# Moving the residual sums before the second FFN from GpSimd's program to VectorE's, in a decoder layer on one core

## What is computed

```
h = x + 0.5 * rms(swiglu(rms(x, g)), g)                 # first FFN
u = rms(h, g);  merged = gateA * attention(u) + gateB * recurrence(u)
h = h + rms(merged @ w_out, mix_post_g)                 # the sum that this case is about
h = h + 0.5 * rms(swiglu(rms(h, ffn2_pre_g)), g)        # second FFN
rms(y, g) = y * rsqrt(mean(y*y) + eps) * g
```

## Time and profile before

| | |
|---|---|
| runs | 2288.19 us median (2286.82, 2288.19, 2291.76) |
| profiled execution | 2288.33 us, span 2286.5 us |
| TensorE busy | 2158.2 us, 94% of the span |
| VectorE busy | 1389.8 us, 61% |
| ScalarE busy | 974.8 us, 43% |
| GpSimd busy | 450.2 us, 20% |
| mean granted clock of TensorE | 0.979 |

### The profile page before, as it was taken

One profiled execution on the slowest core, in us unless ns is written; L12 is line 12 of the kernel. 1 busy time (PEld: TensorE's weight loads), 2 busy tenths in 40 slices (PEclk: granted clock), 3 DMA queues, 4 the chain that ended last, 5 costly groups with the idle time before them and its releaser, 6 DMA issues.

```text
span 2286.5 us, 25908 instructions
## 1 busy us (share of the span) xinstructions
PE 2158.2 (94%) x9837; PEld 1789.6 (78%) x9837; DVE 1389.8 (61%) x1718; ACT 974.8 (43%) x1543; POOL 450.2 (20%) x453
## 2 busy tenths in 40 slices
PE   4999999999998999999999888998699999999997
PEld 3888788878886888888887777776588888888885
DVE  7668865557576666212214887677856766557666
ACT  5333333344353776311324666445433333334343
POOL 5123320000032221000012555215312321000012
PEclk8999999999999999999999999999799999999998
DMA  3345442253442212222310100455135453216334
GB/s 120 93 156 185 157 166 70 70 198 98 151 148 80 57 46 54 69 70 85 106 43 25 27 14 10 166 189 175 55 98 185 164 197 123 72 51 221 101 134 142
DMA packets 220293, 249.85 MB, mean 109 GB/s; under 512 B 24261, under 2 KB 161546, under 8 KB 220170
## 3 DMA queue, kind: packets, MB, share of 16 engines
q1 hardware_dynamic: 220170, 248.19, 33.3%
HBM read 192.06 MB, written 55.57 MB: 108 GB/s over the span
## 4 chain that ended last, share of the span: by engine, by line
PE 85%; DVE 6%; ACT 3%; POOL 2%; issue 2%; DMA 1%; POOLq 0%; SPq 0%; ACTq 0%; DVEq 0%
PE ps L88 28%; PE ps L90 27%; PE ps L89 27%; PE ps L2172 1%; PE ps L2140 1%; DVE ff_t L98 1%; POOL a_rot L2057 1%; PE ps L357 1%; ACT a_probs L2116 1%; DVE a_s L2106 1%; DVE a_pt L98 1%; DVE entry_y L342 0%; DVE w_lo L98 0%; DMA w_raw<-in_w_out_dram 0%; ACT entry_squares L282 0%
## 5 line engine op out<-in xcount | busy, mean ns | idle before, releaser
L98 DVE TENSOR_TENSOR ff_w_lo<-ff_raw,ff_w_hi 128x512 fp32r<-128x512 f32 x264 | 209.8, 798 | 171.9 <-ACT ff_w_hi L94 171.8
L88 PE MATMUL ps<-ff_t,ff_w_hi 128*128 128x512 f32 x704 | 276.4, 393 | 18.8 <-DVE ff_t L98 18.8
L89 PE MATMUL ps<-ff_t,ff_w_hi 128*128 128x512 f32 x704 | 275.9, 392 | 0.0
L90 PE MATMUL ps<-ff_t,ff_w_lo 128*128 128x512 f32 x704 | 275.6, 392 | 0.0
L94 ACT ACTIVATE ff_w_hi<-ff_raw 128x512 fp32r<-128x512 f32 x264 | 164.9, 627 | 180.7 <-PE ps L90 173.5
L88 PE MATMUL ps<-d_b_hi,d_a_hi 128*128 128x512 f32 x608 | 237.5, 391 | 3.7 <-DVE d_a_lo L98 3.7
L98 DVE TENSOR_TENSOR w_lo<-w_raw,w_hi 128x1024 fp32r<-128x1024 f32 (+2 forms) x81 | 93.9, 1164 | 237.1 <-ACT w_hi L94 237.0
L90 PE MATMUL ps<-d_b_hi,d_a_lo 128*128 128x512 f32 x608 | 236.7, 389 | 0.0
L89 PE MATMUL ps<-d_b_lo,d_a_hi 128*128 128x512 f32 x608 | 236.7, 389 | 0.0
L88 PE MATMUL ps<-ff_b,ff_w_hi 128*128 128x512 f32 x528 | 209.6, 397 | 8.1 <-ACT ff_u2x L692 5.0
L90 PE MATMUL ps<-ff_b,ff_w_lo 128*128 128x512 f32 x528 | 208.2, 394 | 0.0
(11 more groups left out here) (296 smaller groups left out, 4365.7 us busy)
## 6 DMA issues: line engine op xcount, KB each, us to landing
ff_raw<-in_ffn_w_gate_dram SPq DMA_DIRECT2D x44, 512.0 KB, 4.0
ff_raw<-in_ffn_w_up_dram SPq DMA_DIRECT2D x44, 512.0 KB, 4.0
d_sums<-in_ffn_w_down_dram SPq DMA_DIRECT2D x44, 512.0 KB, 4.1
sums_scratch<-d_sums SPq DMA_DIRECT2D x88, 256.0 KB, 2.6
w_raw<-in_w_in_dram SPq DMA_DIRECT2D x32, 512.0 KB, 4.0
d_raw<-sums_scratch SPq DMA_DIRECT2D x24, 512.0 KB, 3.3
w_raw<-in_w_out_dram SPq DMA_DIRECT2D x24, 512.0 KB, 4.3
spill_scratch<-ff_st SPq DMA_DIRECT2D x44, 256.0 KB, 3.1
```

What stands on the lines that cost most here:

```text
L88: pe.matmul(out, lh, rh, start=start, stop=False, skip_group_check=go_on)
L89: pe.matmul(out, lh, rl, start=False, stop=False, skip_group_check=go_on)
L90: return pe.matmul(out, ll, rh, start=False, stop=stop, skip_group_check=go_on)
L98: return nc.vector.tensor_tensor(lo, src, as_f32(hi), ALU.subtract)
```

## The change

The flag `add` of `norm_pool` and `norm_dve` says which of the two issues the sum of step 2. For the tiles 0 to 4, which are handled beside groups 1 and 2 of the output projection, GpSimd's program is now told not to (it had the default, True), and VectorE's is told to (it had the default, False). The other calls stay.

```diff
--- before.py
+++ after.py
@@ -2864,7 +2864,7 @@
                 for g in range(1, 3):
                     for k in range(DK):
                         for s, q in out_steps(g, k):
-                            entry(f2, s, q)
+                            entry(f2, s, q, False)
                 for z in range(11):
                     for s, q in row(z, 5, NT):
                         entry(f2, s, q, False)
@@ -2993,7 +2993,7 @@
                                 op.evacuate_dve(dve, t)
                         if g > 0:
                             for s, q in out_steps(g, k):
-                                entry(f2, s, q)
+                                entry(f2, s, q, True)
                         if k < 6 and 8 + 8 * g + k + 3 < len(outs):
                             w.lo(dve, outs[8 + 8 * g + k + 3])
                     if g < 2:
```

## The result

| | before | changed |
|---|---|---|
| median of 20 runs | 2287.98 us | 2292.79 us |
| ratio, 95% interval | | 1.0023 (1.0016 to 1.0030) |
| profiled execution, span | 2288.33, 2286.5 us | 2288.75, 2287.0 us |

The ratio compares all executions of the two kernels and is not the quotient of the two medians; one of the 20 executions of before took 4893 us and is left out of it (without that one the median of before is 2287.76 us). By the ratio the change makes the kernel slower by 0.23%, which is 5.3 us (3.7 to 6.9); by the medians it is 4.8 to 5.0 us. The forecast was +4.1 us, 2292.3. The likeliest of the three classes had been "no change within 0.2%" at 0.54 against 0.42 for slower; the measured ratio lies 0.03% on the other side of that bound, but the bound is inside its interval, so the timing does not decide between the two.

A forecast was written before the change was run, and what follows sets the result against it. TensorE is 94% busy; in output projection group 2 a ring of ScalarE, GpSimd and VectorE steps sets the time. 0.3 + 2.5 + 0.1 + 1.9 - 0.7 = +4.1 us on 2288.2 gives 2292.3, range 2289.5 to 2295.2.

The forecast's parts named there:

- the three terms of group 2: Output projection group 2: later sums of tiles 2, 3 and 4, at +2.5, +0.1 and +1.9 us.
- The clock term: PE's slow clock after its waits: less of it falls on matmuls, -0.7 us, bounds -1.9 and +1.7.
- Tiles 0 and 1, +0.3: Group 1: sums later in VectorE's queue delay PE's tail of group 1 by 0.3 us, bounds 0 and +0.4.
- Tile 2, +2.5: Group 2: the sum queues behind a w_lo waiting for PE-released w_hi, so its square starts 2.5 us later.
- Tile 3, +0.1: Group 2: pre-gain of tile 2, then the sum, take 2.45 us from the root's end; +0.1 us.
- Tile 4, +1.9: Group 2: sum behind w_lo, low part, pre-gain and GpSimd's whole at the port; +1.9 us, bounds +0.8 and +2.1.
- Rival C: VectorE goes first at the port, so tile 4 costs +0.8; all in all +3.0 us, 2291.2; chance 0.13.
- rival B: The clock gives nothing back or takes more: +4.8 to +6.5 us, 2293.0 to 2294.7; chance 0.25.
- The signs of being wrong: Tile 2's square before 1576, tile 4's sum taking 1.2, or slow stretches moving by more than a microsecond.
- Rival D, the faster engine: VectorE's sum is 1.17 us shorter, twice in the chain: -2.3 us, 2285.9; chance 0.12 shared with another rival.

The follow-up runs named there:

- Run 3: Only the sums of tiles 0 and 1 moved from GpSimd to VectorE, against the kernel before; median 2287.01 us, ratio 0.9994.
- run 2: Only the sum of tile 4 moved from GpSimd to VectorE, against the kernel before; median 2290.65 us, ratio 1.0011.
- run 8: Only tile 4's sum on VectorE, ahead of the pre-gain of tile 3 instead of behind it; against the kernel before, median 2288.16 us, ratio 1.0001.
- run 1: Only the sum of tile 2 moved from GpSimd to VectorE, against the kernel before; median 2291.24 us, ratio 1.0009.
- run 5: Changed kernel with the sums of tiles 0 and 2 directly behind their own post-gain; against the kernel before, median 2289.86 us, ratio 1.0010.
- run 4: Changed kernel with all five sums on VectorE directly behind their own post-gain; against the kernel before, median 2283.79 us, ratio 0.9978.
- run 7: All sums stay on GpSimd, each ahead of the root of the tile before; against the kernel before, median 2290.07 us, ratio 1.0010.

## Why the prediction was right

The time, 2292.79, is 0.5 us from the forecast, and in the changed kernel's profile the three terms of group 2 came out on the paths that were given for them. The clock term did not hold, the path at tiles 0 and 1 was another, and the 0.5 us is less than the timing can tell.

*Tiles 0 and 1, +0.3.* The distance from post-gain to tail grew by 0.57, but not on the path that I gave, over VectorE's own queue: the w_lo now waits 1.57 us for a w_hi, and that for a load, as this row of ScalarE shows. The load was issued at 1540.12 and used at 1545.92, 5.8 us later, where before it took 4.5.

```profile
1545.92 1.06 ACT L94 ACTIVATE w_hi<-w_raw 128x1024 fp32r<-128x1024 f32 x1 [3.15 <-DMA w_raw<-in_w_out_dram]
```

The prediction named this load and took it as 0.4 late. It is issued hardly later (12.87 us behind the post-gain of tile 0, before 12.75) but takes longer: 5.6 to 5.9 us from issue to use in the three profiles with these two sums on VectorE in step 2, 4.5 to 5.1 where group 1 is that of before. Why it takes longer no run shows. Run 3 (ratio 0.9994) and the scatter of this group in runs 2 and 8 leave the term unproved; it is small either way.

*Tile 2, +2.5.* 2.52 in the changed kernel, 2.50 in run 1, and 0 in run 5, where only the place is undone. *Tile 3, +0.1.* 0.12. *Tile 4, +1.9.* 1.79, and 1.77 in run 2; that the whole goes first at the port is seen in the 2.29 of the sum there, in run 5 too, and in the 1.22 of run 8, where the sum stands ahead of the whole. Rival C is out. The waits of PE came as said, 3.21 before the turn of tile 3 (3.3 forecast); before that of tile 4 it is 1.41, not over 2, since the chunk ahead of it ran slow (granted clock 0.50), which the prediction had weighed under rival B and called hidden in that wait. It was: the piece up to the tail is 9.40, before 9.42.

The Trainium skill (SBUF — State Buffer, Who interferes with whom) gives the port to the instruction issued first, for its whole length; the trace agrees in both directions, GpSimd's sum held by w_lo (3.31) and VectorE's held by whole (2.29).

*Clock, -0.7.* The profile has +1.46 before the w_hi, -1.58 in the tail and -0.5 after it, -0.6 in all. But run 1 has the same late w_hi, with the same program ahead of it, and across the ten profiles the distance from restart to w_hi goes from 4.42 to 7.33. Before stands between the two, so in one execution the clock moves the time by 1.5 us either way, and over many it need not give anything back. That this one profile shows -0.6 beside the -0.7 of the prediction is chance. The timed 5.3 us (3.7 to 6.9) has room for 4.1 and lies nearer to the terms without the clock, which measured 0.57 + 4.41 = 5.0. If a term was mis-sized it is this one; what it is over many executions no run shows.

*The signs of being wrong.* Two of the three that the prediction names came up. The square of tile 2 starts at 1574.95, before 1576; this says nothing, since that execution reached the post-gain of tile 0 3.95 us early, and absolute times of two executions should not have been compared. The slow stretches did move by more than a microsecond, twice and in opposite directions (+1.46 and -1.58); this one counts, against the clock term. The third, a sum of tile 4 of 1.2, did not.

*Rival D, the faster engine.* It falls for this change, but run 4 shows that it named something real: with the sums on VectorE and put where their inputs are ready, the ruler is 2.7 us shorter and the kernel 5.0 us faster, and run 7 shows that GpSimd's sums, put early, do not give that. How much of it is the shorter sum and how much the relief of the port was not taken apart. My condition for it, that tile 2's w_hi be released sooner, was too narrow; it is enough to put the sum on the other side of the w_lo.

## What to carry to other kernels

Moving an instruction to a faster engine moves it into another queue. Ask what stands ahead of it there and what that waits for: here a sum of 1.22 us cost 2.5 us behind a w_lo that waited for TensorE, and nothing in front of it. When work changes engines, place it anew by when its inputs are ready and its result is wanted; here another order turned 5 us lost into 5 us gained, with the same instructions on the same engines. And measure a change this small as a distance between two events of the chain: single executions of the kernel before lay between 2283.64 and 2291.76 us, which is more than the effect. The distance leaves out what happens outside it, as the clock in the tail, so the timing of many executions has to stand beside it.

## What the runs showed of the hardware

A wait between GpSimd and VectorE, read as one at the port that they share, moves on when the order changes: 2.29 us on the sum in run 2, on the pre-gain behind it in run 8. And how much of the work behind PE's restart runs at the slow clock differs between executions: from the restart to the release of the same w_hi, with the same instructions in between, it took 4.42 us at the least (run 7, granted clock 1.00 from 1566 to 1572) and 7.33 at the most (the changed kernel, 0.50 from 1564 to 1570).
